# Two mixer layers and a sparse-attention block: dense head rows ahead of the scan's features, fewer stage ends, and identity products in TensorE's waits

## What is computed

```python
h = x * (1.0 + scale[:, None]) + shift[:, None]
(a_q, a_i, a_ff, a_fb, b_q, b_k, b_v, c_q, c_k, c_v, d_q, d_k, d_v, g_lat) = jnp.split(h @ w_in, SPLIT_AT, axis=-1)
...
qB = apply_rope(rms_norm(split_heads(b_q, GA_HEADS), ga_qn), rope64)
...
y = jnp.concatenate([y_a, y_b, y_c, y_d], axis=-1) * jax.nn.silu(g_lat)
x_new = layer_norm(alpha * x + gate[:, None] * (y @ w_out), ln_g, ln_b)
```

## Time and profile before

| | us |
|---|---|
| median of 3 runs | 2256.44 (2253.99 to 2260.58) |
| the profiled execution | 2254.11 |
| its span, first to last instruction | 2252.2 |
| PE busy | 2035.5 (90% of the span) |
| DVE busy | 1139.5 (51%) |
| ACT busy | 756.5 (34%) |
| POOL busy | 54.3 (2%) |
| mean granted TensorE clock | 0.962 of full speed |

### The profile page before, as it was taken

One profiled execution on the slowest core, in us unless ns is written; L12 is line 12 of the kernel. 1 busy time (PEld: TensorE's weight loads), 2 busy tenths in 40 slices (PEclk: granted clock), 3 DMA queues, 4 the chain that ended last, 5 costly groups with the idle time before them and its releaser, 6 DMA issues.

```text
span 2252.2 us, 26284 instructions
## 1 busy us (share of the span) xinstructions
PE 2035.5 (90%) x9904; PEld 1375.5 (61%) x9904; DVE 1139.5 (51%) x2524; ACT 756.5 (34%) x1622; POOL 54.3 (2%) x96
## 2 busy tenths in 40 slices
PE   5888998999879888889899797999899997999999
PEld 2644655555444454555555445886588886887887
DVE  2285173545553827427456557995444434333333
ACT  2222233544341122223554414326423224222222
POOL 2000000000000100000000020000000000000000
PEclk9999999999999999999999998998999998999999
DMA  8111111010372211201010232331133332333331
GB/s 270 27 37 38 47 38 38 1 38 1 113 257 80 63 28 38 61 24 57 19 38 1 93 80 65 94 85 29 48 94 94 96 101 56 94 95 94 101 94 66
DMA packets 152685, 157.28 MB, mean 70 GB/s; under 512 B 5676, under 2 KB 114384, under 8 KB 152560
## 3 DMA queue, kind: packets, MB, share of 16 engines
q1 hardware_dynamic: 146672, 137.91, 20.3%
q0 software_dynamic: 5888, 17.68, 2.9%
HBM read 151.37 MB, written 4.19 MB: 69 GB/s over the span
## 4 chain that ended last, share of the span: by engine, by line
PE 71%; DVE 19%; ACT 5%; issue 3%; DMA 2%; POOL 1%; DVEq 0%; ACTq 0%; SPq 0%; POOLq 0%
PE psum L740 14%; PE psum L1185 9%; PE psum L1187 9%; PE psum L1186 9%; PE psum L752 5%; PE psum L915 5%; PE psum L767 5%; PE psum L948 3%; PE psum L929 3%; DVE stats L2004 2%; PE psum L703 2%; DVE arena L2267 2%; ACT arena L1460 1%; PE psum L785 1%; PE psum L716 1%
## 5 line engine op out<-in xcount | busy, mean ns | idle before, releaser
L740 PE MATMUL psum<-arena 128*128 128x512 f32 (+1 forms) x1280 | 469.5, 523 | 0.0
L1293 ACT ACTIVATE arena<-psum 128x384 f32<-128x384 f32 (+7 forms) x520 | 205.2, 423 | 683.9 <-PE psum L703 250.4
L1185 PE MATMUL psum<-part,part 128*128 128x512 f32 x992 | 390.0, 393 | 14.8 <-DVE part L2386 7.0
L1187 PE MATMUL psum<-part,part 128*128 128x512 f32 x992 | 389.0, 392 | 0.0
L1186 PE MATMUL psum<-part,part 128*128 128x512 f32 x992 | 389.0, 392 | 0.0
L740 PEld LDWEIGHTS psum<-arena 128*128 128x128 f32 x1280 | 243.7, 194 | 193.3 <-issue 176.6
L2382 DVE TENSOR_TENSOR part<-arena,part 128x1024 fp32r<-128x1024 f32 x112 | 137.1, 1225 | 250.3 <-ACT part L1293 250.3
L1293 ACT ACTIVATE part<-arena 128x1024 fp32r<-128x1024 f32 (+1 forms) x198 | 174.2, 913 | 218.2 <-PE psum L1187 148.2
L1185 PEld LDWEIGHTS psum<-part,part 128*128 128x128 f32 x992 | 187.9, 189 | 56.8 <-issue 13.9
L2004 DVE TENSOR_REDUCE stats<-psum 128x1 f32<-128x768 f32 (+6 forms) x208 | 138.8, 708 | 159.0 <-PE psum L915 157.6
L1186 PEld LDWEIGHTS psum<-part,part 128*128 128x128 f32 x992 | 188.1, 190 | 39.6
(11 more groups left out here) (269 smaller groups left out, 2016.0 us busy)
## 6 DMA issues: line engine op xcount, KB each, us to landing
arena<-in_w_in SPq DMA_DIRECT2D x75, 512.0 KB, 4.1
arena<-in_w_mlp SPq DMA_DIRECT2D x64, 512.0 KB, 3.9
arena<-in_w_ada SPq DMA_DIRECT2D x48, 512.0 KB, 5.7
arena<-in_w_gate SPq DMA_DIRECT2D x32, 512.0 KB, 4.0
arena<-in_w_out SPq DMA_DIRECT2D x24, 512.0 KB, 3.7
arena<-in_w_in SPq DMA_DIRECT2D x16, 256.0 KB, 3.1
arena<-in_w_branch SPq DMA_DIRECT2D x8, 512.0 KB, 5.0
arena<-in_x POOLq DMA_DIRECT2D x4, 512.0 KB, 9.0
```

The lines of the kernel that those rows point to most:

```text
L740: mm = pe.matmul(bank(b)[:, c0:c1], lhs[:, k, m * P:(m + 1) * P], ring.view(tag, l, k // 2)[:, k % 2, c0:c1], start=k == 0, stop=k == kt - 1)
L1185: pe.matmul(dst, lo, x_hi_, start=first, stop=False)
L1187: return pe.matmul(dst, hi, x_hi_, start=False, stop=last)
L1293: return act.activation(dst, src, ACT.Copy)
```

## The change

- **Order.** `b` comes first at t = 0 and `d` first at t = 1, in the ring's list and in `stream`; the six tiles of that kind (`AHEAD = TT`) are taken on PE, ACT and DVE before `scan_inputs`. PE waits for each token tile of h before a `b` tile.
- **Gate.** `g0` moves from beside the attention to the end of the stream at t = 1, in the same pieces. Beside the attention stay `g1` and `ada`. `beside_steps` gives the proportion: 14 stream steps for the 14 scan steps at t = 0; at t = 1 30 (layer 0) or 22 (layer 1).
- **Stage ends** after the start and after `layer_end(0)` go; the others are numbered anew.
- **Banks.** The scan's q features go to banks 6 and 7.
- **Masks.** One `copy_predicated` does two groups; PE's bank frees and the next levels wait for both.
- **Gains.** `load_gains(0)` is issued right behind the x tiles, `load_gains(1)` behind the residual loads of layer 0's end. The small sums for lambda stay at the head of a layer on DVE; ACT's exponential of them moves behind `scan_inputs` of t = 0 and the rest of it behind the scan of t = 0. ACT waits for the stored rows before it writes q and f in layer 1.
- **Identity products.** `keep_going(b, n)` issues n products of the identity by itself (128 columns) into bank b, ahead of a wait, at ten places outside the scans. Nothing reads them.

Calls that are alike on the other engines and the renumbered stage waits are left out below.

```diff
     for l in range(DEPTH):
         w = a["w_in"][l]
         for t in range(2):
+            tag, c = (("b", C_B), ("d", C_D))[t]
+            rows((tag, l), w, c, 512)
             for name, c in (("q", C_AQ), ("f", C_FF), ("b", C_FB)):
                 cols(("hg", l, t, name), w, c + P * t)
             if t == 0:
                 rows(("ai", l), w, C_AI, 256)
-                rows(("b", l), w, C_B, 512)
                 rows(("c", l), w, C_C, 512)
             else:
                 rows(("cv", l), w, C_CV, 256)
-                rows(("d", l), w, C_D, 512)
         rows(("g0", l), w, C_G, 512)
         rows(("g1", l), w, C_G + 512, 512)
         if l < DEPTH - 1:
...
 def stream_tiles(t):
-    return [(tag, m) for tag in (("ai", "b", "c") if t == 0 else ("cv", "d")) for m in range(TT)]
+    return [(tag, m) for tag in (("b", "ai", "c") if t == 0 else ("d", "cv")) for m in range(TT)]
+AHEAD = TT
+def beside_steps(l, t):
+    return 2 * TT + 2 if t == 0 else TT + 4 * last_q_of(l)
+def feature_bank(name, s):
+    return 6 + s if name == "q" else s
...
+    def keep_going(b, n):
+        for _ in range(n):
+            pe.matmul(bank(b)[:, 0:P], ident[:], ident[:], start=True, stop=True)
     def transposes(src, n_blocks, b, width=P):
...
-            open_bank(s)
+            b = feature_bank(name, s)
+            open_bank(b)
             for k in range(KT):
-                mm = pe.matmul(bank(s)[:, 0:t1 - t0], ring.view("hg", l, t, name)[:, k, :], h_t[:, k, t0:t1], start=k == 0, stop=k == KT - 1)
+                mm = pe.matmul(bank(b)[:, 0:t1 - t0], ring.view("hg", l, t, name)[:, k, :], h_t[:, k, t0:t1], start=k == 0, stop=k == KT - 1)
             names = [("hg", l, t, name, s)] + ([("weights", ring.number("hg", l, t, name))] if last else [])
             mm.then_inc(mm_done(*names), 1)
-            bank_free(s, [scan_dve.at("q", l, t, s) if name == "q" else scan_act.at(name, l, t, s)])
+            bank_free(b, [scan_dve.at("q", l, t, s) if name == "q" else scan_act.at(name, l, t, s)])
     def scan(l, t):
         banks = scan_banks(l)
...
             pe.wait_ge(*scan_dve.at("e", l, t, level))
-            level_mm(level, E[:, 1], E[:, 0], lambda g: scan_dve.at("level", l, t, level, g))
+            level_mm(level, E[:, 1], E[:, 0], lambda g: scan_dve.at("level", l, t, level, g - g % 2, g - g % 2 + 1))
             yield True
         pe.wait_ge(*scan_dve.at("e", l, t, FIRST_STATE))
...
+            if tag == "b":
+                pe.wait_ge(*h_act.at("h", l, m))
+                pe.wait_ge(*h_dve.at("h", l, m))
             product_tile(tag, l, m, b, h_t, KT, m == TT - 1, c0, WIDTH[tag], m == 0)
             bank_free(b, [rows_act.at("row", tag, l, m)])
             if p >= 2 and tiles[p - 2][0] in HEADS:
                 turn_keys(l, *tiles[p - 2])
             yield True
-        for tag, m in tiles[-2:]:
+        for tag, m in tiles[-2:] if t == 0 else []:
             turn_keys(l, tag, m)
+        if t == 1:
+            yield from gate(l, 0)
+    def gate(l, n):
+        tag = "g%d" % n
+        for m in range(last_q_of(l)):
+            open_bank(0)
+            yield from product_pieces(tag, l, m, 0, h_t, m == last_q_of(l) - 1, m == 0)
+            bank_free(0, [gate_act.at("row", tag, l, m)])
     def gate_and_ada(l):
-        for tag in ("g0", "g1"):
-            for m in range(last_q_of(l)):
-                open_bank(0)
-                yield from product_pieces(tag, l, m, 0, h_t, m == last_q_of(l) - 1, m == 0)
-                bank_free(0, [gate_act.at("row", tag, l, m)])
+        yield from gate(l, 1)
         if l < DEPTH - 1:
             yield from ada(later_ada(l))
...
                 prepare(l, i + 2, banks)
+            if l == 2 and i == 0:
+                open_bank(map_bank(l, 0, 0))
+                keep_going(map_bank(l, 0, 0), 6)
             if i < len(steps_):
                 scores(l, i)
...
             if half == 0:
+                if m == 0:
+                    keep_going(b, 16)
                 pe.wait_ge(*gy_dve.at("y", l, m))
...
                 open_bank(2 + half)
+                if v == 0 and half == 0:
+                    keep_going(2, 7)
                 pe.wait_ge(*bc_dve.at("diag", l, v, half))
...
+            beside = stream(l, t)
+            for _ in range(AHEAD):
+                next(beside)
             scan_inputs(l, t)
-            beside = stream(l, t)
             next(beside)
-            alongside(scan(l, t), 14, beside, 20 if t == 0 else 13)
-            stage_end(2 + 4 * l + t)
-        alongside(attend(l), len(attention_steps(l)) + 4, gate_and_ada(l), 8 * last_q_of(l) + (16 if l < DEPTH - 1 else 0))
-        stage_end(4 + 4 * l)
+            alongside(scan(l, t), 14, beside, beside_steps(l, t))
+            stage_end(1 + 3 * l + t)
+        alongside(attend(l), len(attention_steps(l)) + 4, gate_and_ada(l), 4 * last_q_of(l) + (16 if l < DEPTH - 1 else 0))
+        stage_end(3 + 3 * l)
         layer_end(l)
-        if l < DEPTH - 1:
-            stage_end(5 + 4 * l)
...
+                if half == 0:
+                    keep_going(b, ((15, 28, 5, 5), (14, 14, 5, 5))[which][m])
                 pe.wait_ge(*rms_act.at("row", which, m))
...
         hi, lo = parts_2(("fm", i))
+        if i == 2:
+            keep_going(b, 6)
         for k in range(KT):
...
             open_bank(2)
+            keep_going(2, 9)
...
+        open_bank(0)
+        keep_going(0, 8)
         for n in range(len(keys) - together):
...
                 open_bank(b)
+                if d == 0 and n == 0:
+                    keep_going(b, 14)
                 pe.wait_ge(*lo_dve.at(("gate", d, n)))
...
             if d == 0:
+                open_bank(2)
+                keep_going(2, 9)
                 pe.wait_ge(*xlo_dve.at("y", KT - 1))
             for n in range(4):
...
             pe.wait_ge(*lo_dve.at(("mlp1", f)))
+            if f == 0:
+                keep_going(b, 7)
             for k in range(KT):
...
         modulate(0, m, stage_x[m])
-    stage_end(1)
     layer(0)
     layer(1)
     block_2_inputs()
-    stage_end(9)
+    stage_end(7)
     attend_2()
-    stage_end(10)
+    stage_end(8)
...
         x.then_inc(h_act(("h", l, m)), 1)
     def scan_inputs(l, t):
+        if l and t == 0:
+            act.wait_ge(*x_stored.at("all"))
         for name, s, t0, t1 in hg_tiles(l):
             act.wait_ge(*mm_done.at("hg", l, t, name, s))
             dst = q_s[:, t0:t1] if name == "q" else f_s[:, 0 if name == "f" else 1, t0:t1]
-            act.activation(dst, bank(s)[:, 0:t1 - t0], ACT.Sigmoid).then_inc(scan_act((name, l, t, s)), 1)
+            act.activation(dst, bank(feature_bank(name, s))[:, 0:t1 - t0], ACT.Sigmoid).then_inc(scan_act((name, l, t, s)), 1)
         act.wait_ge(*scan_dve.at("inputs", l, t))
         act.activation(f_s[:], f_s[:], ACT.Ln).then_inc(scan_act(("ln", l, t)), 1)
...
                 i = raw_turn(l, tag, m)
-                if i >= 2 and i % (2 * TT) >= 2:
+                if i >= 2:
                     before = raw_user(l, i - 2)
                     act.wait_ge(*turn_done.at("k", before[1], l, before[2]))
...
                 modulate(l + 1, m)
     def layer(l):
-        act.wait_ge(*lam_dve.at("sums", l))
-        act.activation(lam[:, 2:4], lam[:, 0:2], ACT.Exp).then_inc(lam_act(("exp", l)), 1)
         for t in range(2):
+            beside = stream(l, t)
+            for _ in range(AHEAD):
+                next(beside)
             scan_inputs(l, t)
-            beside = stream(l, t)
+            if t == 0:
+                act.wait_ge(*lam_dve.at("sums", l))
+                act.activation(lam[:, 2:4], lam[:, 0:2], ACT.Exp).then_inc(lam_act(("exp", l)), 1)
...
                 decays(level + 1)
-            for g in range(scan_groups(l) if level < FIRST_STATE else 0):
+            for g in range(0, scan_groups(l) if level < FIRST_STATE else 0, 2):
                 lo_tile, hi_tile = group_tiles(g)
-                n = hi_tile - lo_tile
-                dve.wait_ge(*scan_mm.at("level", l, t, level, g))
+                n, b = hi_tile - lo_tile, banks["level", level, g]
+                dve.wait_ge(*scan_mm.at("level", l, t, level, g + 1))
                 if level == 0:
-                    dve.wait_ge(*scan_act.at("base", l, t, g))
+                    dve.wait_ge(*scan_act.at("base", l, t, g + 1))
                 else:
-                    dve.wait_ge(*scan_dve.at("level", l, t, level - 1, g))
-                dve.copy_predicated(att[:, g % 2, lo_tile:hi_tile, :], bc(level_mask[:, level, :], 1, [P, n, P]),
-                                    bank(banks["level", level, g])[:, 0:n * P].rearrange("p (j n) -> p j n", n=P)).then_inc(scan_dve(("level", l, t, level, g)), 1)
+                    dve.wait_ge(*scan_dve.at("level", l, t, level - 1, g, g + 1))
+                mask = level_mask[:, level, :].unsqueeze(1).unsqueeze(1).to_broadcast([P, 2, n, P])
+                dve.copy_predicated(att[:, :, lo_tile:hi_tile, :], mask,
```

(51 more changed lines are left out.)

52 lines of the change are left out of this document (25 added, 27 removed).

## The result

| | before | after |
|---|---|---|
| median, 5 runs each on one chip | 2258.03 (2253.99 to 2261.20) | 2245.82 (2243.95 to 2248.21) |
| ratio | | 0.9934, 95% interval 0.9918 to 0.9950 |
| the profiled execution, its span | 2254.1, 2252.2 | 2248.2, 2246.4 |

The account below looks back on a forecast made before the run. TensorE, working 90% of the span, was taken as the bound. Terms -22.5 - 27.5 + 39.5 + 26 - 34 - 18 - 8 = -44.5 us from 2254.1 gave 2209.6, or 2212 on the median's footing; range 2188 to 2238.

Parts of the forecast that it names:

- The holes of t = 0: PE's idle time in both layers' t = 0 stages: closing it takes them from 195 to 174 and 179 to 153 us.
- PE stays the bound, barely: Run of `b` tiles at t = 0: DVE has 6.5 us per tile against PE's 6.9 plus 0.1.
- the added work: `g0` pieces at t = 1, 41 and 27.5 us; with changes in holes, stages +39.5 us (layer 0) and +26 (layer 1).
- The moved table load: ACT's exponential for lambda, put behind the logarithm, takes the 1.283 us load from before t = 0's first level's exponentials.
- The gains come before they are needed, covered by the run's first tile: t = 0: early gain loads cost nothing; uncovered they would cost again up to 6.8 us.
- of 27.5, 7.5 back in `c` and 10.5 in the rest: Layer 1's attention: of 27.5 us of gate pieces moved away, 18 us come back.
- Those steps now take about 5.5 on average: Attention's 16 `c` steps: above a 4.6 us loop, each can give about 0.5 to 0.9 us.
- Rival D: Attention: softmax loop already sets nearly every step, none of the 69 us returns; slower, 2264 us; chance 0.04.
- Rival B: Attention gives back only 30 us, the loop and copies between transposes in `b` and `d` ending last; 2234; chance 0.15.
- rival C: Identity products too short to keep the clock or too long for their waits: +6 instead of -8, 2226; chance 0.15.
- 16 (3.8) and 7 (1.7) products: Layer end 0: identity products fit waits of 3.90 and 2.13 us; -3 us there, -2 in layer 1.
- -5 after some latency: Second attention: six identity products, 1.4 us, fit its first waits and save 5 us of work at half clock.

Follow-up runs that it names:

- e1: The changed kernel with POOL issuing the ten gain loads only once the columns of scale are summed; 2239.4 us, ratio 0.9899 to the kernel before.
- e12: Changed kernel with late gains, old t = 1, identity products at selected second-block sites plus six at the second attention's start; 2202.2 us, ratio 0.9742 to the kernel before.
- e2: The changed kernel without any of its 204 identity products; 2238.8 us, ratio 0.9906 to the kernel before.
- e5: The changed kernel with gain loads later, t = 1 of both layers as before, and no identity products; 2217.1 us, ratio 0.9794 to the kernel before.
- e3: The changed kernel with t = 1 of both layers as before the change, t = 0 staying new; 2221.5 us, ratio 0.9817 to the kernel before.

## Why the prediction was wrong

**What held.** The holes of t = 0: forecast 174 and 153 us for the two stages, measured 176.9 and 154.8, and e1 to e12 all keep layer 0's at 175.5 to 177.2. "PE stays the bound, barely" held too. At t = 1 the added work was over-priced by 10.0 us (+33.9 and +21.6 for +39.5 and +26), which by luck hid as much of the other misses; 0.7 of it is a reading, since a level costs DVE 5.8 us by the earlier trace rows (115.91 to 121.70) and not 5.9. The granted clock there is 1.00, and PE idles 5.8 us where I had the idling of seven levels on top of a bare tail. The moved table load went where it was meant to: in the changed kernel ACT loads for the logarithm at 127.01 and for lambda at 129.81, and none stands before the first level's exponentials. What that gave no run parts from the rest of t = 0.

By the Trainium skill ("VectorE: DVE Perf Modes", The TRN2 errata) a PSUM source costs 120 cycles, 0.125 us, per instruction. The trace now bears on it, for a mask instruction over two banks takes 1298 ns and two over one bank took 717 each, 136 less for the instruction saved; with half the width 716 for two of 430, 144 less: near the page's figure in both. It changed no term: VectorE ends last only in a few levels.

**The start.** The failing step is "The gains come before they are needed, covered by the run's first tile". I asked when they are needed and not what they pass on the way: without the stage end POOL runs 37 us ahead and its loads meet the weight stream. e1 shows the whole price, 8.0 us.

**Layer 1's attention.** The step is "of 27.5, 7.5 back in `c` and 10.5 in the rest". The rest gave 9.0. `c` gave nothing and took 6.7, for two reasons. "Those steps now take about 5.5 on average" was the wrong length: they took 5.4 us in layer 0 but 5.1 in layer 1. The chain allowed layer 1 some 6 us at most (8 by the 4.6 of the earlier trace rows), a bound I could have computed: 16 steps of 4.7 are 75, and the trace had 81.7. And I priced the emptier steps at an unchanged clock. After the change they take 5.5 us each in layer 1, which the prediction itself had named as a sign of being wrong.

Rival D had the mechanism (the softmax loop sets the steps, the pieces only fill it) at a chance of 0.04 and for both layers; it was true for half the steps of one layer. It decides between 321 and 340 us there. Rival B had the size: 30 us back, where the two attentions gave 32.8. Its mechanism is not what happened, for the steps of `b` and `d` gave nearly what I had for them.

In layer 0, with 24 pieces of `g1` and the `ada` products still there, 30.6 of 34 came back. The same term fell short: the 16 steps of `c` went from 86.8 to 82.0 us, 4.8 for a forecast of 8, and the rest gave 25.8 for 26.

**The identity products.** "An identity product is two, 0.24 us, and 0.48 at 1.2 GHz" was right, and so was the delay at m = 0 (+3.5 for +2.5). "16 (3.8) and 7 (1.7) products" at the layer ends was not: they begin after a wait that has taken the clock. And "-5 after some latency" for the second attention has nothing behind it: no profile with the products is shorter than 71.1 us, and it was 71.0 before. As a whole +7 (e2), or +8.9 by the rows of the table, where the sum had -8: rival C's +6.

**The second attention's 4.4 us** go with the granted clock: with the same instructions that stage ran at 0.80 to 0.93. What decides between them stays open, as does the scatter of e5; no run here isolates it.

**The size.** The sum -44.4 missed by 38.5 us, and its range of 25 to each side was built from rivals about one term, the attention's return. By term it is 19.2 us in the attentions, 16.8 in the identity products, 7.3 at the start and 5.1 at t = 0, less 10.0 at t = 1. The start had no rival. B and C were each priced alone; both sizes came true at once, and the forecast with the 22 us of B and the 14 of C would have been 2248, outside the range and within 3 us of the result (the misses at the start, at t = 0 and at t = 1 nearly cancel).

## What to carry to other kernels

Before work is moved away from a stage, bound what the stage can give: the number of its steps times the length of its longest dependent chain is a floor, and only what the stage takes above it can come back; if the work also filled waits, part of what it gives back is lost to a lower clock. When a barrier is removed, follow every queue that it held, DMA queues too, to the stretch in which its work now lands. Split a change by stages and try the halves: here the kernel with new t = 0 and old t = 1 beat the whole change by 24 us by the medians, 26 by the ratios.

## What was unexpected

Ten loads of 2 to 64 KB halved the rate of a 512 KB stream for 10 us (188 GB/s for 390) at an unchanged DMA share, and cost 8 us. Two profiles can differ by 4 to 7 us in a single stage whose instructions are alike, with a granted clock of 0.80 or 0.91 (78.3 us in e3's second attention, 71.9 in e12's, the instructions alike), while whole runs of one kernel mostly lie within 0.4%.
